# Twenty-four modulation tiles beside the time mixing, not 32, in a two-layer encoder kernel

## The reference, cut to what matters

```
mod_all = silu(c) @ ada_w + ada_b                       # for each layer
layer 0: shift1, scale1, gate1, shift2, scale2, gate2 = split(mod_all[0], 6)
   x = x + gate1 * time_mixing(rmsnorm(x) * (1 + scale1) + shift1)      # w_o is its last matrix
   x = x + gate2 * swiglu(rmsnorm(x) * (1 + scale2) + shift2)           # w1, w3, w2
layer 1: the same with sparse attention in the place of time mixing
out = rmsnorm(x) * final_norm
```

## Time and profile before

| | |
|---|---|
| median of 3 runs | 2695.6 us (2694.96 to 2698.59) |
| profiled execution | 2698.5 us, its span 2696.9 us |
| PE, DVE, ACT busy | 96%, 71%, 46% of the span |
| granted TensorE clock, mean | 0.986 |
| DMA | 641 MB, 238 GB/s on average |
| modulation products on DVE | 144 of 128x2048, 2.28 us each; 64 of 128x1024, 1.21 us each |
| mixing | about 386 to 724 us of the span |
| third down projection of layer 0 | about 1496 to 1566 us |

### The profile page before, as it was taken

How to read it: one execution, slowest core, us unless ns; L and a number is a source line. 1 busy time by engine, 2 the same in 40 slices (tenths; PEclk the granted TensorE clock), 3 DMA queues, 4 the chain that set the end, 5 groups by cost and what they waited for, 6 DMA issues and landing times.

```text
span 2696.9 us, 53365 instructions
## 1 busy us (share of the span) xinstructions
PE 2582.7 (96%) x20124; PEld 2264.0 (84%) x20124; DVE 1917.0 (71%) x2661; ACT 1239.7 (46%) x1894; POOL 46.3 (2%) x83
## 2 busy tenths in 40 slices
PE   7999998888899999999999999999999999999999
PEld 6788887877787888888888878897788888888887
DVE  6868747877587777777777776587887655555556
ACT  2245554444445444444444454444454444444444
POOL 2000020000000000000000000000000000000000
PEclk9999999999999999999999999999999999999999
DMA  9998775444296888888887768666788666666653
GB/s 401 414 324 307 260 254 167 159 143 135 78 306 215 283 282 291 282 283 274 291 277 273 230 217 284 221 212 209 243 281 281 213 191 185 189 191 190 187 164 125
DMA packets 452403, 640.98 MB, mean 238 GB/s; under 512 B 22304, under 2 KB 411552, under 8 KB 431392
## 3 DMA queue, kind: packets, MB, share of 16 engines
q1 hardware_dynamic: 448512, 626.35, 69.2%
q0 software_dynamic: 3744, 12.59, 1.3%
HBM read 624.18 MB, written 14.68 MB: 237 GB/s over the span
## 4 chain that ended last, share of the span: by engine, by line
PE 69%; DVE 3%; ACT 1%; issue 0%; ACTq 0%; DVEq 0%
PE ps L1820 44%; PE ps L1824 22%; PE ps L1430 1%; PE ps L1423 1%; DVE wlo L1804 1%; ACT whi L1799 0%; DVE nt L131 0%; DVE act L144 0%; DVE ada_ring L1866 0%; PE ps L1414 0%; PE ps L1457 0%; PE ps L1465 0%; PE ps L1581 0%; PE ps L1447 0%; PE ps L1474 0%
## 5 line engine op out<-in xcount | busy, mean ns | idle before, releaser
L1804 DVE TENSOR_TENSOR wlo<-raw,whi 128x1024 fp32r<-128x1024 f32 (+1 forms) x736 | 866.1, 1191 | 448.9 <-ACT whi L1799 447.0
L1820 PE MATMUL ps<-act,whi 128*128 128x512 f32 x3528 | 1108.5, 396 | 1.4 <-DVE act L144 1.4
L1799 ACT ACTIVATE whi<-raw 128x1024 fp32r<-128x1024 f32 (+1 forms) x736 | 746.7, 1030 | 655.2 <-PE ps L1824 649.4
L1824 PEld LDWEIGHTS ps<-act,wlo 128*128 128x128 f32 x3528 | 662.8, 188 | 156.6
L1824 PE MATMUL ps<-act,wlo 128*128 128x256 f32 x3528 | 693.2, 278 | 0.0
L1820 PE MATMUL ps<-hid,whi 128*128 128x512 f32 x2176 | 681.8, 394 | 7.6 <-DVE wlo L1804 6.4
L1820 PEld LDWEIGHTS ps<-act,whi 128*128 128x128 f32 x3528 | 537.4, 189 | 2.0 <-DVE wlo L1804 1.0
L1824 PEld LDWEIGHTS ps<-hid,wlo 128*128 128x128 f32 x2176 | 410.9, 189 | 90.1
L1824 PE MATMUL ps<-hid,wlo 128*128 128x256 f32 x2176 | 433.8, 280 | 0.0
L1820 PEld LDWEIGHTS ps<-hid,whi 128*128 128x128 f32 x2176 | 333.0, 189 | 10.1 <-issue 4.3
L1866 DVE SCALAR_TENSOR_TENSOR ada_ring<-ada_ring,silu 128x2048 f32<-128x2048 f32 x128 | 292.3, 2284 | 11.0 <-DMA ada_ring<-in_ada 11.0
(11 more groups left out here) (275 smaller groups left out, 2188.2 us busy)
## 6 DMA issues: line engine op xcount, KB each, us to landing
raw<-in_f_w SPq DMA_DIRECT2D x480, 512.0 KB, 4.6
ada_ring<-in_ada SPq DMA_DIRECT2D x144, 1024.0 KB, 7.6
raw<-in_a_w_rkv SPq DMA_DIRECT2D x96, 512.0 KB, 7.8
ada_ring<-in_ada SPq DMA_DIRECT2D x64, 512.0 KB, 4.2
raw<-in_b_w_in SPq DMA_DIRECT2D x56, 512.0 KB, 3.9
raw<-in_f_w SPq DMA_DIRECT2D x64, 384.0 KB, 3.9
first_ring<-in_ada SPq DMA_DIRECT2D x16, 1024.0 KB, 12.7
raw<-in_a_w_o SPq DMA_DIRECT2D x32, 512.0 KB, 7.2
```

Of the source, the lines that this page charges most:

```text
L1799: self.nc.scalar.activation(self.whi[:, u % SPL, 0:n], self.raw[:, u, 0:n], ACT.Copy).then_inc(self.s("hi_ready"), 1)
L1804: self.nc.vector.tensor_tensor(self.wlo[:, u % SPL, 0:n], self.raw[:, u, 0:n], self.whi[:, u % SPL, 0:n].bitcast(F32), SUB).then_inc(self. ...
L1820: self.nc.tensor.matmul(self.ps[0:c1 - c0, banks[b], :], hi[:, kk, c0:c1], src[:, k].rearrange("p a t -> p (a t)"), start=k == 0, stop=False)
L1824: last = self.nc.tensor.matmul(self.ps[0:c1 - c0, banks[b], T:2 * T], lo[:, kk, c0:c1], src[:, k, 0, :], start=False, stop=k == ktotal - 1)
```

## The change

Mixing makes three tiles an iteration (`TILES = 3`, six halves), tiles 48 to 71, so piece 3 and half of piece 4. The output projection makes tiles 72 to 79 and finishes piece 4. Tiles 80 to 87, which were its own, are made in pairs 0 to 3 of the first up projection of the first feed-forward, and what follows shifts. Counted by pairs, two products are new in pair 0 of that up projection, and six are new in pairs 1 to 3 of the third down projection; all other pairs have two products as before. With three tiles an iteration the slots no longer repeat each iteration, so the index `m` runs through and SP's loop is written out. Halves 5 and 6 stood together on DVE ahead of `grow(... "W32" ...)`, half 7 ahead of `grow(... "W64" ...)`; half 5 remains.

```diff
         mods0 = self.mods_made
-        self.mods_made += KT // 2
+        TILES = 3
+        FINISHED = -(-KT // TILES)
+        self.mods_made += FINISHED
...
-        TILES = 2 * KT // L
         HALVES = 2 * TILES
...
         def ada_half(dve, i, n):
 
-            dve.wait_ge(s(f"half_loaded{n % 4}"), i * 32 + 16 * (n // 4 + 1))
-            nc.vector.scalar_tensor_tensor(place(n), place(n), 1.0, self.silu[:, (n % 2) * W:(n % 2 + 1) * W], MUL, MUL,
+            m = i * HALVES + n
+            dve.wait_ge(s(f"half_loaded{m % 4}"), 16 * (m // 4 + 1))
+            nc.vector.scalar_tensor_tensor(place(m), place(m), 1.0, self.silu[:, (n % 2) * W:(n % 2 + 1) * W], MUL, MUL,
                                            accum_out=self.parts[:, n:n + 1]).then_inc(s("ada_half"), 1)
...
                 for n in ns:
-                    if not (isinstance(i, int) and i == 0 and n < 4):
-                        sp.wait_ge(s("ada_half"), i * HALVES + (n - 3))
-                    sp.dma_start(place(n), view[bass.ds(i * TILES + (ADA_FIRST + n // 2), 1), :, (n % 2) * W:(n % 2 + 1) * W]
-                                 .rearrange("a p k -> p (a k)")).then_inc(s(f"half_loaded{n % 4}"), 16)
+                    m = i * HALVES + n
+                    if m >= 4:
+                        sp.wait_ge(s("ada_half"), m - 3)
+                    sp.dma_start(place(m), view[ADA_FIRST + m // 2, :, (n % 2) * W:(n % 2 + 1) * W]).then_inc(s(f"half_loaded{m % 4}"), 16)
...
             def body(i, more):
-                ada(i, 6, 7)
                 ada(i + 1, 0, 1, 2, 3)
                 gates(i)
...
-            with sp.Fori(0, L - 2) as i:
+            for i in range(L - 2):
                 body(i, True)
             body(L - 2, False)
-            ada(L - 1, 6, 7)
             gates(L - 1)
...
-                parts = self.parts[:].rearrange("p (m h) -> p m h", h=2)
+                parts = self.parts[:, 0:HALVES].rearrange("p (m h) -> p m h", h=2)
...
-                tt("mod_ready", self.mod[:, at], self.mod[:, at], self.pv[:, bass.ds(i * TILES + (PV_ADA + ADA_FIRST), TILES)], ADD)
+                if i < FINISHED:
+                    lo, hi = i * TILES + ADA_FIRST, min((i + 1) * TILES, KT) + ADA_FIRST
+                    tt("mod_ready", self.mod[:, lo:hi], self.mod[:, lo:hi], self.pv[:, PV_ADA + lo:PV_ADA + hi], ADD)
...
-                adas(i, 5, 6)
+                adas(i, 5)
                 grow(i, "W32", 1, SUB, "P4")
                 if prep:
                     prep_c(i + 1, 1 - q)
-                adas(i, 7)
                 grow(i, "W64", 3, SUB, "W32")
...
-        phases = [Linear(self, w_o, 4, self.ffn_first(0), hid, None, AddGated(self, 2, True), [(0, 4, 80)], first_loaded=EARLY,
+        phases = [Linear(self, w_o, 4, self.ffn_first(0), hid, None, AddGated(self, 2, True), [(0, 4, 72)], first_loaded=EARLY,
                          begun=3)]
-        phases += self.ffn(0, [[(1, 5, 88), (5, 8, 96)], [(0, 4, 102)], [(0, 1, 110), (1, 8, 112)], [(0, 1, 126), (1, 4, 128)],
-                               [(0, 5, 134), (5, 6, 144)], [(0, 1, 146)]], dsa_in)
+        phases += self.ffn(0, [[(0, 8, 80)], [(0, 4, 96)], [(0, 4, 104), (4, 8, 112)], [(0, 4, 120)], [(0, 6, 128)],
+                               [(0, 2, 140), (2, 4, 144)]], dsa_in)
```

## The result

| | before | after |
|---|---|---|
| median | 2695.6 us, 11 runs (2691.9 to 2698.59) | 2701.89 us, 11 runs (2700.52 to 2707.83) |
| profiled execution, span | 2698.5, 2696.9 us | 2701.73, 2699.9 us |

The ratio of after to before is 1.0026, its 95% interval 1.0018 to 1.0035, so +7.0 us with an interval of 4.9 to 9.4. The forecast was 2703.8 us, from a sum of +8.2. The medians themselves differ by 6.3. The total came out nearly right; its parts did not all.

A forecast was written before the change was run, and what follows sets the result against it. It took TensorE to bound the kernel outside mixing, and a chain of small steps inside. Terms 8.7 + 0.5 - 1.0 = +8.2 us on 2695.6 gave 2703.8 us, range 2696.5 to 2709.0.

The forecast's parts named there:

- Part 4: Third down projection of the first feed-forward: six added products overfill DVE and delay the stage's end, 8.7 + 0.5 us.
- DVE in its order: Third down projection: adding up DVE's queue, it reaches the last additions to x 7.3 us later.
- the loop: Third down projection: DVE's extra wait of 0.27 us after each of four sums in the loop is now paid, +1.1 us.
- the finishing addition: Third down projection, between pairs 1 and 2: an addition with a wait on either side, estimated at +0.3 us.
- the root's chain: Behind the third down projection: half clock after PE's idle time makes DVE wait longer for the root, +0.5 us.
- Rival (a): Third down projection: PE's lead of split units absorbs the delay, only the last product shows; +0.5 us, 2696.1 us, chance 0.10.
- Parts 2 and 3: Output projection and first up projection: the moved tiles and two new products in pair 0 cost 0, upper bound 0.5 us.
- Part 1: Mixing: removing 16 half products gains only 1.0 us, in the last iteration; other iterations keep their spacing.
- rival (c): Mixing: less load traffic shortens PE's stops for issue by a tenth, -4.0 us, 2699.8 us; chance 0.11.
- The -1.0 for DVE's work: Mixing's last iteration: without half 6, the 1.01 us hole in PE's work closes, -1.0 us.
- Rival (b): Mixing is set by DVE after all, so its removed work counts in full; -9.2 us, 2686.4 us, chance 0.06.
- Rival (d): Third down projection: loads arrive late, 1 us on five of them, +5 us, 2708.8 us; chance 0.07.

The follow-up runs named there:

- down_six: The kernel before, with only the six products added in pairs 1 to 3 of layer 0's third down projection; 2703.85 us against 2695.04, ratio 1.0029.
- mixing_only: The changed mixing with the later phases of the kernel before, tiles 72 to 79 not made; 2694.24 us against 2697.53, ratio 0.9984.
- the larger experiment: The kernel before, all 64 mixing products made but only the first two halves loaded; -14.6 us, ratio 0.9946.
- the direct runs: The kernel before, mixing's halves 6 and 7 loaded but not multiplied (-5.1, -3.0 us), or multiplied but not loaded (-4.0, -3.2 us); each run twice.
- the relief: The changed kernel, with four of the six products moved out of the third down projection to later phases; 2695.73 us, ratio 1.0000 to before.
- tail: The changed kernel, with the last product of three projections moved behind the last additions to x; 2694.01 us, ratio 0.9999 to before.
- relief_tail: The changed kernel, with four products moved out of the third down projection and last products placed behind the additions to x; 2689.53 us, ratio 0.9975 to before.

## Why the prediction was right, and where it was not

**Part 4, the stage that decides: right.** Forecast were 7.3 for DVE in its order, 1.1 for the loop, 0.3 for the finishing addition and 0.5 for the root's chain, 9.2 in all; the trace shows 8.67, and down_six shows 8.64 without the rest of the change. Term by term: DVE is 8.2 us late where 8.7 was forecast. The loop's four groups cost 9.14 - 8.90 = 0.24 us more each, 1.0. The finishing addition costs nothing: the group that holds it (sums at 1530.61 and 1539.77) took 9.16 us, as the loop's others; the estimate of 0.3 is the term that was too large. The root came after 2.82 us of waiting and not 2.29: +0.5. PE's holes for splits are 0.21 to 0.60 us, at most about the 0.57 by which DVE was said to be short. Rival (a) is refuted by the same rows: the small holes are there, yet what sets the end is DVE's queue ahead of L357, and the lead of split units did not shield it.

**Parts 2 and 3: right.** Output projection +0.1 us, within its scatter, first up projection 0.0.

**Part 1: the step that failed is "Less traffic could shorten PE's own stops; I take 0 for that too and keep it as a rival".** In its place the runs show about 4 us: stops of 36.7 us on average in the traces with 24 tiles, where those with 32 had 41.0, and a quarter of the 14.6 that all the loads cost is 3.65. So rival (c) happened, at about its price of 4.0 (a tenth of the stops), and it happened beside the forecast's terms, not instead of them; the two should have been summed as one case. The -1.0 for DVE's work stands: the hole in the last iteration shrank by 1.1 us, and in after PE's waits for DVE and ACT are 1.3 us fewer (0.4 on the average of the traces). That half 6 becomes idle time was right where I looked, in one iteration, and I inferred the others from it. "Shorter iterations refute part 1" was the test named, and mixing_only met it.

**The sum.** By the runs it is -4.3 (mixing_only) and +8.7, +4.4, where the ratio gives +7.0 with 4.9 as the near end. These don't quite meet. Mixing's -4.3 has 2.5 us of uncertainty either way, and the same part read as after against down_six is only 0.8. So it was in part luck that the total of 8.2 came so close: with mixing at -4.3 the forecast would have been 9.2 - 4.3 = +4.9, the low end of what was measured. Rival (b) is refuted as a case on its own: all 64 products, 64 x 1.15 = 73.6 us of DVE work, are worth 8.1 us, a ninth. Rival (d) did not show: DVE has no wait for a load in its list for the stage.

**Still open.** That the gain of the 16 halves is mostly the loads' rests on the averages of three and five traces and on quartering the larger experiment, which supposes that the effect grows evenly; the direct runs could not resolve it. Why a fetch starts later beside loads is open as well. The Trainium skill (Runtime: NRT & Kernel Launch, Instruction fetch mechanics) describes blocks of 256 instructions whose crossing is mostly hidden. The packets of 16,384 bytes, one for 250 matmuls and weight loads, fit such blocks; but in this stage only about half of the crossings are hidden, and the others stopped PE for 1.4 us each in before and for 1.3 us without the loads.

## What to carry to other kernels

Count work on an idle-looking engine in its order, not by its share: DVE had 29% of its time free and six products of 2.2 us still cost 8.7 us, because each half pair had 0.57 us too little room and the stage's last additions stand at the end of that queue. Work that is to fill gaps belongs behind the last link of such a chain, where the engine waits in any case; moving one product there gave 2.0 to 2.2 us at each place, and with the relief it turned the slower change into a faster kernel. And a stage whose bound engine stops for "issue" may pay for bulk loads that run beside it, even when nobody waits for their data: see whether each stop ends just behind a packet of the instruction queue.

## What the chip showed that I had not expected

**Loads beside a dense instruction stream.** Mixing used 44% of the DMA time, and PE waited for no load. Yet taking away loads whose data only DVE's filler work reads shortened the kernel by 14.6 us, with PE's stops down by 11.9: its instruction fetches took no less time without the loads, but on average started sooner in its work.

**The granted clock after the same idle time is not the same.** The forecast tied the half clock to the idle time ahead of the sum of squares, from one place. The same chain stands at two places (behind the output projections of layer 0 and layer 1) with an idle time of 2.42 to 2.45 us in twelve of the kernels, all but tail and relief_tail. Its four matmuls showed half clock throughout in 4 of the 24, a fall in the middle in 12, and full clock in 8. The fall came in all 24: by the clock's own record between 0.3 us ahead of the first of them and 2.3 us behind its start. Two places of one execution of after:

```profile
815.32 2.08 PE L1892 MATMUL ps<-tmp,ones 128*128 128x256 f32 x4 [2.42 <-ACT tmp L343]
...
1942.98 0.70 PE L1892 MATMUL ps<-tmp,ones 128*128 128x256 f32 x2 [2.42 <-ACT tmp L343]
```

Before had them nearly the other way round: full clock at the first place, and at the second a fall 0.47 us behind the start of the first matmul. At half clock DVE waited 2.74 us for the root in after (818.48), at full clock 2.26 in before (824.59). So a change of about 0.5 us there between two profiles may be chance and no effect of the change. Behind 5.6 us of idle time, in after and in down_six, and behind 3.40 in tail, it was half each time:

```profile
1568.00:1573.00 5.00, 2.08 (x4) 1.03 (x5) 2.18 (x6) 2.60 (x6) 0.00 (x0) 0.50 0.03 10
```

The Trainium skill (TensorE: Matmul & The Clock Gate, What's actually happening) says that an idle TensorE falls to half its clock; the rows agree for the longer idle times and show both levels after the same short one.
